# Attention scores from array parts: products of 64 or 32 partitions instead of zero-padded keys

## What is computed

```python
# second_block, h = rms_norm(x); every head has 64 channels, the halves of the differential heads have 32
o_moba = softmax(mq @ mk.T / 8 - slope * dist, causal) @ mv                 # 4 heads, own keys
o_slc  = softmax(nq @ nks.T / 8 - slope * dist, causal) @ nvs               # 4 heads, one shared key head
o_win  = softmax(nq @ nkw.T / 8 - slope * dist, causal) @ nvw               # 4 heads, one shared key head
p      = softmax(d1 @ k1.T * s) - lam * softmax(d2 @ k2.T * s); o_diff = p @ dv   # 4 heads, two maps each
o_swa  = softmax(sq @ sk.T / 8 - slope * dist, window 128, sink) @ sv        # 4 heads, 2 key heads
```

## Time and profile before

| | us |
|---|---|
| median of 3 runs | 954.94 (954.74 to 955.85) |
| the profiled execution, its own time | 954.55 |
| its span, first to last instruction | 952.7 |
| TensorE busy in it | 934.7 (98%) |
| VectorE busy | 677.9 (71%) |
| ScalarE busy | 477.7 (50%) |
| GpSimd busy | 228.4 (24%) |

### The profile page before, as it was taken

The page is one execution under the profiler, slowest core; times in us unless marked ns, Lnnn a source line. Parts: engine busy times, 40 slices in busy tenths (PEclk is TensorE's granted clock), DMA queues, the critical chain, the costliest instruction groups (busy, mean ns, idle before and its releaser), DMA issues.

```text
span 952.7 us, 15307 instructions
## 1 busy us (share of the span) xinstructions
PE 934.7 (98%) x6006; PEld 835.1 (88%) x6006; DVE 677.9 (71%) x1265; ACT 477.7 (50%) x941; POOL 228.4 (24%) x123
## 2 busy tenths in 40 slices
PE   9999999999999989999999999999999999999997
PEld 8879999979999878888888889998888888888886
DVE  6735987658555877685666655876888888788884
ACT  6433223564544486524434645585745455445542
POOL 3112112233400317323351165421111200312220
PEclk9999999999999999999999999999999999999999
DMA  8535333134333546655446345213545555454621
GB/s 311 191 133 177 133 134 123 56 111 139 128 133 105 199 162 225 224 184 207 178 177 220 133 144 199 100 52 116 209 142 201 188 198 213 180 205 177 221 89 45
DMA packets 23495, 153.93 MB, mean 162 GB/s; under 512 B 2800, under 2 KB 3568, under 8 KB 5888
## 3 DMA queue, kind: packets, MB, share of 16 engines
q1 hardware_dynamic: 22704, 150.80, 44.0%
q0 software_dynamic: 576, 2.10, 0.6%
q10 hardware_dynamic: 144, 0.07, 0.0%
HBM read 151.38 MB, written 1.05 MB: 160 GB/s over the span
## 4 chain that ended last, share of the span: by engine, by line
PE 91%; DVE 4%; ACT 3%; issue 1%; DVEq 0%; ACTq 0%
PE pb L496 89%; PE pb L499 2%; DVE wl L505 1%; ACT FA L502 1%; DVE FA L505 1%; ACT wh L502 1%; DVE R L511 1%; ACT R L502 1%; DVE X L511 0%; DVE FA L511 0%; DVE FA L508 0%; ACT st L502 0%; DVE wh L520 0%; ACT L502 0%; DVE st L523 0%
## 5 line engine op out<-in xcount | busy, mean ns | idle before, releaser
L496 PE MATMUL pb<-R,wh 128*128 128x256 f32 (+2 forms) x2224 | 551.5, 327 | 5.2 <-ACT R L502 2.5
L496 PE MATMUL pb<-R,wl 128*128 128x256 f32 (+1 forms) x1512 | 423.5, 282 | 0.0
L496 PEld LDWEIGHTS pb<-R,wh 128*128 128x128 f32 x2224 | 372.8, 190 | 46.5 <-ACT R L502 4.0
L505 POOL TENSOR_TENSOR wl<-raw,wh 128x1024 fp32r<-128x1024 f32 (+1 forms) x81 | 198.7, 2459 | 666.4 <-ACT wh L502 498.2
L505 DVE TENSOR_TENSOR wl<-raw,wh 128x1024 fp32r<-128x1024 f32 (+1 forms) x197 | 251.1, 1300 | 80.0 <-ACT wh L502 78.6
L496 PEld LDWEIGHTS pb<-R,wl 128*128 128x128 f32 x1512 | 285.6, 189 | 1.9
L502 ACT ACTIVATE wh<-raw 128x1024 fp32r<-128x1024 f32 (+1 forms) x229 | 233.4, 1046 | 65.5 <-PE pb L496 58.9
L496 PE MATMUL pb<-wh,R 128*128 128x512 f32 (+2 forms) x724 | 234.7, 389 | 4.4 <-DVE FA L505 1.6
L502 ACT ACTIVATE FA<-pb 128x256 f32<-128x256 f32 (+7 forms) x239 | 96.1, 418 | 174.4 <-PE pb L496 161.1
L496 PEld LDWEIGHTS pb<-wh,R 128*128 128x128 f32 (+1 forms) x724 | 134.3, 186 | 38.1 <-DVE FA L505 2.0
L496 PE MATMUL pb<-wl,R 128*128 128x512 f32 (+2 forms) x372 | 144.2, 388 | 0.0
(11 more groups left out here) (118 smaller groups left out, 516.5 us busy)
## 6 DMA issues: line engine op xcount, KB each, us to landing
raw<-in_w SPq DMA_DIRECT2D x137, 1024.0 KB, 4.8
X<-in_x SPq DMA_DIRECT2D x2, 512.0 KB, 4.2
raw<-in_w SPq DMA_DIRECT2D x2, 512.0 KB, 6.6
post<-in_ffn_post SPq DMA_DIRECT2D x2, 512.0 KB, 5.6
post<-in_w POOLq DMA_DIRECT2D x2, 512.0 KB, 4.4
FA<-in_w POOLq DMA_DIRECT2D x2, 512.0 KB, 4.0
out<-X SPq DMA_DIRECT2D x4, 256.0 KB, 2.0
cst<-in_cst SPq DMA_DIRECT2D x1, 799.0 KB, 12.5
```

Source lines behind the costliest of these rows:

```text
L496: return self.real.matmul(*a, **k) if self.real else self
L505: return self.real.tensor_tensor(*a, **k) if self.real else self
```

## The change

Heads are worked in groups of two (`GROUPS`): two heads of one query tile, one head of each of the two `swa` tiles, or the two maps of one differential head. A new step `scores` of a group has TensorE's part for both maps: its six products take only the 64 (or, for `df`, 32) partitions of their own head, and alternate between the two maps. Each map has one bank for all its three products, kept until its `score` step, which only VectorE still has. The keys have no zeros any more: `KEYS` has six tiles, `df` reads the projection itself, ScalarE makes one copy instead of two scaled ones (four activations fewer in all), the eight multiplications of GpSimd are gone, and SyncE moves half as much (4 copies of 64 KB instead of 8). VectorE waits once per map instead of twice. `MADE` and all strings of `MIX` are new: over all 276 units d goes from 166 to 165, p from 62 to 63, v from 31 to 32, q from 17 to 16; in `maps` the letters go from d 6, p 6, v 4, q 2 to d 11, p 5, v 1, q 1.

```diff
@@ constants
-    put("rows", np.stack([p < 64, p >= 64] + [p // 32 == i for i in range(4)], 1))
+    put("rows", np.stack([p < 64, p >= 64], 1))
@@ segments()
-    for h in range(4):
-        jobs.append(plain(("slc", h)) + plain(("win", h)) + [("cmp_value", h)] + ([("join", 2 + h // 2)] if h % 2 else []))
...
+    def two(g):
+        a, b = GROUPS[g]
+        return [("scores", g), ("score", a), ("exp", a), ("score", b), ("exp", b), ("p_turn", a), ("value", a), ("p_turn", b), ("o_out", a),
+                ("value", b), ("o_out", b)]
+    for n in range(2):
+        jobs.append(two(("slc", n)) + two(("win", n)) + [("cmp_value", 2 * n), ("cmp_value", 2 * n + 1), ("join", 2 + n)])
...
+GROUPS = {(m, n): [(m, 2 * n), (m, 2 * n + 1)] for m in ("slc", "win", "moba") for n in range(2)} \
+    | {("df", h): [("df1", h), ("df2", h)] for h in range(4)} | {("swa", n): [("swa", 2 * n), ("swa", 3 - 2 * n)] for n in range(2)}
+GROUP_OF = {m: (g, i) for g, ms in GROUPS.items() for i, m in enumerate(ms)}
...
-    "maps": "a........db.a.ec.dbaggecf.d.gbf.aagceaifgf.fbaici.ghii.e.dh.efbcdahja.ie.hahjg.cehb.jkdbmc.le.hf"
+    "maps": ".....a..bcc..b.b.caecbbeaebec..bcbaeaecca.cdfbd.fdffggd.fgf.acegdcd.bggb..d.afhbhbcchghb.hiihcb."
...
@@ the map tables in program()
+            r64 = slice(b0, b0 + 64)
-            MAPS["moba", h] = dict(q=mq[:, n, :], k=KEY["moba", h], of=[("evac", "mq", n), ("evac", "mk", n)], bias=(0, h),
+            MAPS["moba", h] = dict(q=mq[r64, n, :], k=KEYS["mk", n][r64, :], of=[("evac", "mq", n), ("evac", "mk", n)], bias=(0, h),
...
-                MAPS[m, h] = dict(q=dqk[:, n, :], k=KEY["df", h, i], of=[("evac", "d", n)], apart=("apart", 2 + n),
+                r32 = slice(b0 + 32 * i, b0 + 32 * i + 32)
+                MAPS[m, h] = dict(q=dqk[r32, n, :], k=dqk[r32, 2 + n, :], of=[("evac", "d", n), ("evac", "d", 2 + n)],
@@ tensor()
-                elif kind == "score":
...
-                    for c in range(2):
-                        nk = 128 + 128 * c
-                        b = bank(("score", m_, c), B5)
-                        for k0 in range(0, nk, 128):
-                            m = e.matmul(b[:, k0:k0 + 128], M["q"][:, 128 * c:128 * c + 128], M["k"][:, k0:k0 + 128], start=True,
-                                         stop=True)
-                        m.then_inc(*pe.up(("score", m_, c)))
+                elif kind == "scores":
...
+                    b = [bank(("scores", g, i), B5, True) for i in range(2)]
+                    for c, k in ((0, 0), (1, 0), (1, 1)):
+                        for i, m_ in enumerate(GROUPS[g]):
+                            M, at = MAPS[m_], 128 * (c + k)
+                            m = e.matmul(b[i][:, at:at + 128], M["q"][:, 128 * c:128 * c + 128],
+                                         M["k"][:, 128 * k:128 * k + 128], start=True, stop=True)
+                            if k:
+                                m.then_inc(*pe.up(("scored", m_)))
...
+                elif kind == "score":
+                    banks.give(("scores", *GROUP_OF[a[0]]))
@@ scalar(), evacuation of the key tiles
-                    for i, m in enumerate(("slc", "win")):
-                        e.activation(KEY[m, i], banks.of(("tm2", 2))[:, 0:256], ACT.Identity,
-                                     scale=rows(i)).then_inc(*act.up(("tm2_out", "k")))
+                    e.activation(KEYS["nk", 0], banks.of(("tm2", 2))[:, 0:256], ACT.Copy).then_inc(*act.up(("tm2_out", "k")))
@@ vector()
-                        e.wait_ge(*pe.at(("score", m_, c)))
+                    e.wait_ge(*pe.at(("scored", m_)))
...
-                        banks.ended(("score", m_, c), dve.now())
+                    banks.ended(bk, dve.now())
@@ gpsimd()
-                elif kind == "evac" and a in (("d", 2), ("d", 3)):
...
-                    for i in range(4):
-                        e.tensor_scalar(KEY["df", 2 * (n - 2) + i // 2, i % 2], dqk[:, n, :], rows(2 + i), None,
-                                        ALU.mult).then_inc(*pool.up(("apart", n)))
@@ sync()
-                    for i, m in enumerate(("slc", "win")):
-                        moved(KEY[m, 1 - i], KEY[m, i], in_nkb[m])
+                    moved(KEYS["nk", 1], KEYS["nk", 0], in_nk)
```

More of the change, by code:

```diff
@@ L568, in program @@
         WL = [sb(f"wl{i}", 1024, FR) for i in range(NBASE)]
-        with nc.sbuf_tensor("keys", [128, 2 * 8 * T1], FP) as keys:
+        with nc.sbuf_tensor("keys", [128, 6 * 256], FP) as keys:
             pass
@@ L595, in program @@
         in_w1 = [signal(f"in_w1_{i}") for i in range(2)]
-        in_nkb, in_s3 = {m: signal("in_nkb_" + m) for m in ("slc", "win")}, [signal(f"in_s3{i}") for i in range(2)]
+        in_nk, in_sk = signal("in_nk"), signal("in_sk")
         out_done = signal("out_done")
-        every = [pe, act, dve, pool, in_xm, in_id, in_gain, in_sm, in_cst, in_lev, out_done] + in_x + in_first + in_slab + in_w1 + list(in_nkb.values()) + in_s3 \
+        every = [pe, act, dve, pool, in_xm, in_id, in_gain, in_sm, in_cst, in_lev, out_done] + in_x + in_first + in_slab + in_w1 + [in_nk, in_sk] \
             + list(in_post.values())
@@ L736, in program @@
         assert o <= NFA, o
+        KEYS = {x: keys[:, 256 * i:256 * i + 256] for i, x in enumerate([("mk", 0), ("mk", 1), ("nk", 0), ("nk", 1), ("sk", 0), ("sk", 1)])}
         PROJ = {("mq", n): mq[:, n, :] for n in range(2)} | {("nkc", 0): nkc} | {("nq", n): nq[:, n, :] for n in range(2)} \
-            | {("d", n): dqk[:, n, :] for n in range(4)} | {("s", n): sqk[:, n, :] for n in range(2)}
+            | {("d", n): dqk[:, n, :] for n in range(4)} | {("s", n): sqk[:, n, :] for n in range(2)} \
+            | {("mk", n): KEYS["mk", n] for n in range(2)} | {("s", 2): KEYS["sk", 0]}
         cols = (slice(0, 128), slice(128, 384))
-        names = [("moba", h) for h in range(4)] + [(m, i) for m in ("slc", "win") for i in range(2)] \
-            + [("swa", n, i) for n in range(2) for i in range(2)] + [("df", h, i) for h in range(4) for i in range(2)]
-        KEY = dict(zip(names, [keys[:, 256 * i:256 * i + 256] for i in range(17)] + more))
-        def rows(i):
-            return C("rows")[:, i:i + 1]
         MAPS = {}
@@ L752, in program @@
             b0, n = 64 * (h % 2), h // 2
[L753 removed]
+            r64 = slice(b0, b0 + 64)
+            MAPS["moba", h] = dict(q=mq[r64, n, :], k=KEYS["mk", n][r64, :], of=[("evac", "mq", n), ("evac", "mk", n)], bias=(0, h),
                                    scale=0.125, v=[TM1[:, c, 64 * h:64 * h + 64] for c in range(2)], vs="tm1_out")
[L755 to L757 removed]
+            for m, gi, voff, moved in (("slc", 1, 0, int(b0 != 0)), ("win", 2, 64, int(b0 == 0))):
+                MAPS[m, h] = dict(q=nq[r64, n, :], k=KEYS["nk", moved][r64, :], of=[("evac", "nq", n), ("tm2_out", "k")],
+                                  moved=in_nk if moved else None,
                                   bias=(1, h), scale=0.125, v=[TM2[:, c, voff:voff + 64] for c in range(2)], vs="tm2_out",
@@ L1315, in scalar @@
                         e.activation(PROJ[use[1:]], b[:, 0:256], ACT.Copy).then_inc(*act.up(step))
-                        banks.ended(use, act.now())
-                    elif name == "mk" or step == ("evac", "s", 2):
-                        e.wait_ge(*pe.at(use))
-                        for i in range(2):
-                            e.activation(KEY["moba", 2 * n + i] if name == "mk" else KEY["swa", i, i], b[:, 0:256], ACT.Identity,
-                                         scale=rows(i)).then_inc(*act.up(step))
                         banks.ended(use, act.now())
```

71 lines of the change are left out of this document (31 added, 40 removed).

## The result

The changed kernel takes **957.12 us** (median of 20 runs, 954.78 to 958.31), the kernel before 955.03 us (20 runs, 954.02 to 956.04). The ratio is 1.0020, 95% interval 1.0014 to 1.0026: slower by 2 us, where 949.4 was forecast. The profiled execution took 957.5 us, its span is 955.7.

A forecast was written before the change was run, and what follows sets the result against it. TensorE, busy 98% of the span, was taken as the bound; -8.0 + 0.9 + 1.4 + 0.6 - 0.4 = -5.5 us against the profiled 954.55 gave 949.05, forecast as 949.4 us, range 947.0 to 953.7.

The forecast's parts named there:

- The new placement: In every segment, weight splits and waits move with no reason for a sign: 0, with 1.5 us either way.
- the serial case: Rival for the scores: the array streams one part at a time, so groups gain nothing; 956.5 us, chance 0.12.
- Groups, -8.0: Scores in `maps`: two parts of the array overlap fully, saving half of 16.0 us over twelve groups.
- Filling, +0.9: Second chain starts and ends up to one record later: 0.11 us for each of eight uninterrupted runs of groups.
- Changes, 0.20 each: Each change of the array's division costs 0.20 us; seven more in all, +1.4 us.
- Bank waits, +0.6: Behind the compressed scores, three groups need six of five banks: `win` 1 waits 0.2 us, the next `p_turn` 0.4.
- elsewhere I count nothing: Bank waits in other places: projections of about 1.4 us or more lie between, so none were counted.
- `tm2_out`, -0.4: Just before `maps`: one ScalarE key copy fewer lets TensorE on 0.37 us sooner.

The follow-up runs named there:

- maps_only: The changed kernel with the old placement in every segment but `maps`; 951.07 us, ratio 0.9963 to the kernel before.
- unit34_quarters: The changed kernel with GpSimd's low part of unit 34 made by four instructions of 256 columns instead of one of 1024; 954.25 us, ratio 0.9989.
- scan_back: The changed kernel with the old placement in `scan` alone; 950.41 us, ratio 0.9955 to the kernel before.
- level_later: The changed kernel with level 2 of the second group of heads in `scan` moved behind the last projection of its stage; 956.19 us, ratio 1.0013.
- unit34_d: The changed kernel with one letter changed: the low part of weight unit 34 made by VectorE instead of GpSimd; 950.62 us, ratio 0.9966.
- one_by_one: scan_back with the six score products of a group issued map by map instead of in turn; 952.86 us, ratio 0.9987 to the kernel before.

## Why the prediction was wrong

The step that failed is one: **"The new placement moves weight splits and waits in every segment. I see no reason for a sign. I take 0, with 1.5 us either way"**. It cost about 5.4 us: the changed kernel's ratio is 1.0020, that of maps_only, which has the old placement outside `maps`, 0.9963. By segment that is 5.5 in `scan` and 0.7 and 0.8 in `out1` and `out2` (against before), less 0.8 in `latent` and a few tenths in `ffn1`; stretches at half clock, which fall in `maps` in the one profile and in `out1` and `out2` in the other, blur the rest by about 1 us. The forecast is missed by 7.4 us in all; the other 2.0, between -5.5 and the -3.5 of maps_only, are 0.6 in `maps` (below) and 1.2 and 0.2 in `out1` and `out2`, where maps_only has before's placement and `out1` a stretch at half clock that before has not. The bound of 1.5 us was taken from waits that were there before; a new wait needs no old one, and I priced it without the clock behind it. I had also put under "slower" only the serial case with a bad placement on top (0.06). A bad placement alone sufficed.

Could it have been read? The order of the changed kernel has decay 1 1 (the products that level 1 2 needs), half a projection, the split of unit 34, a `p`, and then level 0 2 and level 1 2 side by side in TensorE's queue. And the trace before already has the mechanism, with VectorE and GpSimd at 152 us:

```profile
152.38 3.57 DVE L505 TENSOR_TENSOR FA<-FA 128x512 f32<-128x512 f32 x3 [0.18 <-PE pb L496]
...
152.55 2.76 POOL L505 TENSOR_TENSOR wl<-raw,wh 128x1024 fp32r<-128x1024 f32 x1 [7.00 <-ACT wh L502]
```

and in the tile's durations (min/median/max in ns), a median of 426 beside a longest of 2873 (the shapes are mixed; the held one has 512 elements, and its like takes 0.69 us):

```profile
L505 DVE TENSOR_TENSOR FA<-FA x122: 161/426/2873, 21.3 to 934.5; 128x256 f32<-128x256 f32 x68, 128x512 f32<-128x512 f32 x32, 128x64 f32<-128x64 f32 x7, 128x8 f32<-128x8 f32 x4
```

Counted over all records, some 48 VectorE operations of the kernel before take over 0.25 us more than the lower quartile of their shape, 71 us in all, and all but one or two of them overlap a GpSimd instruction. In the changed kernel it is 39 and 58 us, fewer and yet dearer, since one of them lies on TensorE's path. The Trainium skill says it outright ("SBUF — State Buffer", section "Who interferes with whom"): a VectorE instruction with two SBUF inputs contends with a GpSimd instruction that reads SBUF, and the second to issue blocks until the first is done. The trace agrees: 0.41 us became 2.56, while of the 124 products of the same size that read one operand from PSUM, 23 lie wholly inside a GpSimd instruction in the changed kernel and none of these takes more than 0.43 (in unit34_quarters the one at 124.39 us is such). I had not looked it up for a change that moves GpSimd's work.

The rest of the sum, by its terms:

- **Groups, -8.0:** right. A group within a run takes 0.67 us, the first of a run 0.87 with its change of division. The prediction weighed this against 0.87 us a group, an estimate from the Trainium skill's 3.07 times for four parts of 512 columns ("TensorE: Matmul & The Clock Gate", Part 3, "Measured speedup vs the span model"); the overlap of two parts at 128 columns is whole, and the measurement decides.
- **Filling, +0.9:** wrong, it is 0. Both chains start within 0.01 us of each other, and the first group of a run costs 0.87 us in all where the forecast has 0.67 + 0.20 + 0.11.
- **Changes, 0.20 each:** right, 0.19 to 0.21.
- **Bank waits, +0.6:** nearly right at the place named, where it is 0.5. At the pace of the first two groups the third (`win` 1) would start at 609.45, and it starts at 609.77; starting anew costs 0.1 more. At the transpose behind, where the forecast has 0.4, no more than 0.1 is lost. Wrong in "elsewhere I count nothing": from one start to the next, in scan_back, the 76 transpose records of `maps` take 9.2 us instead of 8.1, and the 120 records of value products 13.3 instead of 12.8. The largest piece is a transpose of the window branch that comes 0.5 us late, behind ScalarE:

```profile
624.16 0.92 PE L508 MATMUL pb<-cst,FA 128*128 128x128 f32 x6 [0.33 <-ACT FA L511]
```

  The softmaxes come in pairs now, and what reads them is served in bursts; that this is the reason is my reading and was not tried apart.
- **`tm2_out`, -0.4:** right. TensorE's wait there fell from 1.4 to 1.0 us.

So `maps` gained 4.1 us where these terms want 4.7 (nine of the changes lie there, 1.8 us; the 0.4 of `tm2_out` lie in `ffn1`). That filling costs nothing would give 0.9 us more, so the waits that were counted as nothing took some 1.5. With the disturbances of `scan` and `out2` away, the whole change measures -5.3 against a forecast of -5.5: partly luck, as 0.6 us too much in `maps` met what the new placement gives elsewhere (0.8 in `latent` and 0.3 in `ffn1`, less 0.7 in `out1`). This says what the new scores can give with another placement, not that the forecast held.

Of the rivals, streaming in series (956.5) came nearest to the number, and the runs exclude it: a group takes 0.67 us and not 1.33. That a number fits says little about its mechanism.

## What to carry to other kernels

When a change re-places steps, price it segment by segment, also where its own subject never comes: compare the starts of the segments in both traces before anything else. Where VectorE makes a product that TensorE waits for, see which GpSimd operation begins just before it in the new order; handing that one unit to VectorE gave back 5.2 us. And a wait of TensorE can cost more than its length: here 2.4 us of waiting brought 3.1 us of half clock, which useless products avoided. Not every wait does: the kernel before has one of 2.0 us, at 343.6, and one of 1.4 at `tm2_out`, and its clock is whole behind both. Look at the clock behind each wait before paying for it.

## What the runs showed of the hardware

- A GpSimd operation that begins 0.35 us ahead of a two-operand VectorE product holds it to the end (2.56 us instead of 0.41); cut into four, it holds it for one quarter (0.94 us).
- Half clock came in stretches of 3.4 or 6.8 us: 6.8 behind waits of 2.7 and 2.5 us (level_later), 3.4 behind one of 1.07, none behind 0.53 or 0.34. The length of the wait does not settle it: waits of 1.6 us (206.8) and 2.0 us (343.6) in the kernel before brought none, the wait of 1.9 us for ScalarE in `out2` brought none in the changed kernel, 3.4 us in scan_back and 6.8 in unit34_d, and the changed kernel falls to half clock at 645.6 with no wait over 0.4 us in `maps` before it. What else decides stays open. So the time varies from run to run: the changed kernel's 20 runs spread over 3.5 us, with a mean granted clock of 0.991 to 0.997, where scan_back's five, all at 0.998, spread over 0.6.
- TensorE starts a product of one part of the array ahead of earlier ones of another part: in one_by_one the second map begins while three of the first map's six records are still to start. The Trainium skill says of parallel parts ("TensorE: Matmul & The Clock Gate", Part 3, "The mechanism") that matmuls start strictly in order; the trace shows otherwise.
